# Two modulation blocks move from TensorE to VectorE, the gate's sums move into the feed-forward part, and the second output ends tile by tile

## The reference

```python
mod = c_act @ w_mod + b_mod          # c_act: 2048, w_mod: 2048 x 12288
mod_c = cc_act @ w_mod + b_mod
sh1, sc1, gt1, sh2, sc2, gt2 = split(mod, 6)
h = rmsnorm(x) * (1 + sc1) + sh1;  hc = rmsnorm(ctx) * (1 + csc1) + csh1
x = x + gt1 * merge_groups(scans(h, hc)) @ w_out
h2 = rmsnorm(x) * (1 + sc2) + sh2
x = x + gt2 * (silu(conv3x3(h2 @ w_gate)) * (h2 @ w_val)) @ w_down
return rmsnorm(x, g_final)
```

## Time and profile before

| | |
|---|---|
| median of 3 runs | 2120.66 us (2119.5 to 2120.87) |
| profiled execution | 2120.52 us, span 2118.7, mean granted clock 0.996 |
| PE busy | 2072.9 us, 98% of the span |
| DVE busy | 1599.7 us, 76% |
| ACT busy | 1034.8 us, 49% |
| POOL busy | 112.0 us, 5% |
| DMA | 501.47 MB, mean 237 GB/s |

### The profile page before, as it was taken

How to read it: one execution, slowest core, us unless ns; L and a number is a source line. 1 busy time by engine, 2 the same in 40 slices (tenths; PEclk the granted TensorE clock), 3 DMA queues, 4 the chain that set the end, 5 groups by cost and what they waited for, 6 DMA issues and landing times.

```text
span 2118.7 us, 29080 instructions
## 1 busy us (share of the span) xinstructions
PE 2072.9 (98%) x10157; PEld 1723.0 (81%) x10157; DVE 1599.7 (76%) x2385; ACT 1034.8 (49%) x1289; POOL 112.0 (5%) x175
## 2 busy tenths in 40 slices
PE   7999999999999999999999999999999999999998
PEld 6777778888887778887888887788888888878886
DVE  5789898867787887787666776578888888875554
ACT  4444445654444544546434555355555545544443
POOL 0011010110101110111000000000000000000000
PEclk9999999999999999999999999999999999999999
DMA  8998889998887999986444347565655656567664
GB/s 310 325 323 294 301 266 345 341 292 288 298 293 256 341 302 381 314 294 189 146 127 122 110 128 247 178 202 177 203 181 183 194 178 190 177 216 232 192 192 141
DMA packets 286328, 501.47 MB, mean 237 GB/s; under 512 B 22906, under 2 KB 114464, under 8 KB 284176
## 3 DMA queue, kind: packets, MB, share of 16 engines
q1 hardware_dynamic: 276320, 468.77, 66.9%
q0 software_dynamic: 9904, 31.32, 5.0%
HBM read 487.35 MB, written 19.75 MB: 239 GB/s over the span
## 4 chain that ended last, share of the span: by engine, by line
PE 51%; DVE 1%; DMA 1%; ACT 0%; issue 0%; ACTq 0%; DVEq 0%
PE gemm_ps L1999 23%; PE gemm_ps L2519 8%; PE ps L2519 7%; PE gemm_ps L2522 4%; PE ps L2522 4%; PE ps L2372 1%; PE ps L2441 1%; DMA w_raw<-in_w_out_dram 1%; DVE w_lo L1163 0%; PE ps L2395 0%; PE ps L2394 0%; PE ps L2355 0%; PE ps L2336 0%; PE ps L2067 0%; PE ps L2317 0%
## 5 line engine op out<-in xcount | busy, mean ns | idle before, releaser
L1163 DVE TENSOR_TENSOR w_lo<-w_raw,w_hi 128x1024 fp32r<-128x1024 f32 (+1 forms) x688 | 828.8, 1214 | 354.5 <-ACT w_hi L737 346.6
L737 ACT ACTIVATE w_hi<-w_raw 128x1024 fp32r<-128x1024 f32 (+1 forms) x688 | 717.3, 1053 | 614.4 <-PE gemm_ps L1999 243.3
L1999 PE MATMUL gemm_ps<-w_hi,a_both 128*128 128x512 f32 x2944 | 952.2, 396 | 11.5 <-DVE a_both L1203 6.2
L1999 PEld LDWEIGHTS gemm_ps<-w_hi,a_both 128*128 128x128 f32 x2944 | 554.5, 188 | 141.8 <-issue 12.9
L1999 PE MATMUL gemm_ps<-w_lo,a_both 128*128 128x512 f32 x1472 | 575.1, 391 | 0.0
L1999 PEld LDWEIGHTS gemm_ps<-w_lo,a_both 128*128 128x128 f32 x1472 | 277.6, 189 | 55.0 <-issue 1.0
L2519 PE MATMUL gemm_ps<-a_both,w_hi 128*128 128x512 f32 x704 | 193.8, 397 | 1.6 <-DVE a_both L1203 1.6
L2519 PE MATMUL ps<-a_both,w_hi 128*128 128x512 f32 x672 | 184.7, 394 | 0.0
L1901 DVE SCALAR_TENSOR_TENSOR acc<-gp,cw,acc 128x256 f32<-128x256 f32 x344 | 151.6, 481 | 19.8 <-ACT acc L1109 6.0
L1348 DVE SCALAR_TENSOR_TENSOR msum<-mraw,cs,msum 128x1024 f32<-128x1024 f32 x120 | 153.4, 1278 | 4.7 <-DMA mraw<-in_w_mod_dram 4.0
L1999 PE MATMUL gemm_ps<-w_hi,ft_hi 128*128 128x512 f32 x344 | 134.1, 390 | 3.2 <-DVE w_lo L1163 3.2
(11 more groups left out here) (437 smaller groups left out, 1770.5 us busy)
## 6 DMA issues: line engine op xcount, KB each, us to landing
w_raw<-in_w_in_dram SPq DMA_DIRECT2D x336, 512.0 KB, 5.0
mraw<-in_w_mod_dram SPq DMA_DIRECT2D x192, 512.0 KB, 6.7
w_raw<-in_w_up_dram SPq DMA_DIRECT2D x336, 256.0 KB, 3.0
w_raw<-in_w_down_dram SPq DMA_DIRECT2D x84, 512.0 KB, 4.3
w_raw<-in_w_out_dram SPq DMA_DIRECT2D x64, 512.0 KB, 5.6
w_raw<-in_w_up_dram SPq DMA_DIRECT2D x24, 512.0 KB, 5.7
fold_d<-msum POOLq DMA_DIRECT2D x8, 512.0 KB, 5.4
x_d<-xres POOLq DMA_DIRECT2D x2, 2048.0 KB, 9.1
```

Source lines behind the costliest of these rows:

```text
L737: act.activation(w_hi[:, slot, :, 0:n], raw[:, slot, :, 0:n], ACT.Copy).then_inc(hi_done, 1)
L1163: dve.tensor_tensor(w_lo[:, slot, :, 0:n], raw[:, slot, :, 0:n], w_hi[:, slot, :, 0:n].bitcast(F32), ALU.subtract).then_inc(lo_done, 1)
L1999: mm = pe.matmul(out[:, rt, 0:n], x[:, chunk0 + k, rt * P:(rt + 1) * P], w[:, slot, kk, 0:n], start=(k == 0 and part == 0), stop=(k == chu ...
```

## The change

1. Two instead of four two-row blocks on PE, so four halves of 16 matmuls instead of eight, spaced 21 units apart. Six on DVE: four beside the projections as before, the last two in the pair stage, in the places where sums 2 and 3 were, one block of eight loads and 32 operations for each sum of 16 loads and 16 operations.
2. Sums 2 to 5 in OUT, the context projections and the first x block; sums 6 and 7 in feed-forward blocks 3 to 18, two rows a block, with buffers and a kept copy of the activations of their own. The loops over feed-forward blocks are unrolled on SP and DVE (those of PE and ACT stay), and the pair loop on SP.
3. POOL's queue follows: all folds of the blocks of the pair stage come before the residual's load; sums 2, 3 and 4 before the low-rank weights (`wlr`); sums 6 and 7 and the gate's bias before the gate's load (`gt2b`).
4. OUT2's last block by tile, as at the kernel's end; `tile_root` in place of `roots`; ACT's and DVE's first two feed-forward units move around it.

The core of the diff:

```diff
-PE_MODS = 4
+PE_MODS = 2
+EARLY_BLOCKS = 4
-PAIR_SUMS = (2, 3)
+FFN_SUMS = (6, 7)
+FFN_FIRST = 3
...
-    places = [13 + 21 * h // 2 for h in range(2 * PE_MODS)]
+    places = [13 + 21 * h for h in range(2 * PE_MODS)]
...
-    first = {0: (99, 12), 1: (114, 13), 4: (8 * B_OUT + 8, 16), 5: (8 * B_CTX + 2, 17),
-             6: (8 * B_CTX + 22, 17), 7: (8 * B_X + 4, 18)}
+    first = {0: (99, 12), 1: (114, 13), 2: (8 * B_OUT + 13, 20), 3: (8 * B_CTX + 4, 20),
+             4: (8 * B_CTX + 27, 20), 5: (8 * B_X + 2, 18)}
...
+            def ffn_sum_unit(b, i):
+                at = 2 * (b + 1 - FFN_FIRST) + (i - 3) // 2
+                if i in (3, 5) and 0 <= at < 2 * KC:
+                    sum_unit(FFN_SUMS[at // KC], at % KC)
...
-            with sp.Fori(0, FB - 1) as i:
-                ffn_units(U_FFN // SLOTS + 2 * i, T * i, T)
+            for b in range(FB - 1):
+                ffn_units(U_FFN // SLOTS + 2 * b, T * b, T, lambda i: ffn_sum_unit(b, i))
...
             sum_store(0)
             sum_store(1)
             gate_bias(2)
-            sum_store(2)
-            sum_leaves(3)
+            row_store(4)
+            row_store(5)
             pool.wait_ge(evac_dve, 12)
             pool.dma_start(xres[:], xv).then_inc(S("xres_in"), 16)
...
-            sum_folds(3)
-            sum_store(4)
             pool.wait_ge(evac_dve, 16)
             pool.dma_start(x1_d, xres[:]).then_inc(S("x1_out"), 16)
-            sum_store(5)
-            sum_store(6)
+            sum_store(2)
+            sum_store(3)
+            sum_store(4)
...
+            for n in FFN_SUMS:
+                sum_store(n)
+            gate_bias(5)
             pool.dma_start(gt2b[:], mod_d[0, 0, 5 * D:6 * D].partition_broadcast(P)).then_inc(S("gt2_in"), 16)
...
             for rt in range(RT):
                 last_square(rt, xres, lambda rt: y[:, rt, (DC - 1) * NBLK:DC * NBLK], 1)
+                splits(U_FFN // SLOTS, rt, rt + 1, ffn=True)
+                act.wait_ge(S("root_out"), rt + 1)
+                for c in range(2):
+                    scaled_tile(rt, c)
...
-                    sum_row(PAIR_SUMS[0] + p // 4, at_unit // 2 - 2)
+                    block_rows(KC * (EARLY_BLOCKS + p // 4) + at_unit // 2 - 2)
...
+                if c == DC - 1:
+                    dve.wait_ge(S("tile_ps"), 1)
+                    last_block(0, xres, c % 2, gtb, sg)
+                    tile_root(0, 1)
+                    dve.engine_nop().then_inc(S("root_out"), 1)
+                    dve.wait_ge(used, U_OUT2 + BU * DC)
+                    last_block(1, xres, c % 2, gtb, sg)
+                    splits(U_FFN // SLOTS, 0, 1)
+                    tile_root(1, 1)
+                    dve.engine_nop().then_inc(S("root_out"), 1)
+                    splits(U_FFN // SLOTS, 1, 2)
+                    continue
...
-            sum_of_parts(1)
-            roots()
...
+                    at = 2 * (b - FFN_FIRST) + (i - 3) // 2
+                    if i in (3, 5) and 0 <= at < 2 * KC:
+                        sum_row(FFN_SUMS[at // KC], at % KC)
...
-            with dve.Fori(0, 9) as n:
-                me.iteration(first, 14 * n)
-                for k in range(2):
-                    ffn_block(2 * n + 2 + k, k)
+            for b in range(2, FB):
+                ffn_block(b, b % 2)
...
                 product(U_OUT2 + BU * c, 0, c % 2, a_hi, a_lo, BU, after=after,
-                        turning=("y", y, KC // 2) if c == 0 else None, ahead=Y_AHEAD)
+                        turning=("y", y, KC // 2) if c == 0 else None, ahead=Y_AHEAD, by_tile=SLOTS if c == DC - 1 else 0)
```

More of the change, by code:

```diff
@@ L173, in row_places @@
     ops, loads = {}, {}
-    steps = ROW_BLOCKS * KC
+    steps = EARLY_BLOCKS * KC
     at = [13 + 82 * j // steps for j in range(steps)]
@@ L199, in sum_places, with turn_of, OPS_AHEAD, LOADS_AHEAD @@
                 fetched = at[j - 4] + 4
-            elif n - 1 in first:
+            elif n - 1 in first and n != EARLY_SUMS:
                 fetched = max(first[n - 1][0] + (12 + j) * first[n - 1][1] // 16 + 4, start - 7 + j)
             else:
-                fetched = start - 6 + 2 * j if n == 0 else 8 * B_OUT + j
+                fetched = start - 6 + 2 * j if n == 0 else 8 * B_OUT + 4 + j
             loads.setdefault((fetched // 8, fetched % 8), []).append(16 * n + j)
     return ops, loads
-def MOD_OUT(m):
-    return 16 * (4 * m + 6 * (m - 1))
+EARLY_SUMS = 2
+MOD_OUT = {1: 16 * (6 + 4)}
+def turn_of(kind, n):
+    order = [("rows", m) for m in range(EARLY_BLOCKS)] + [("sum", m) for m in range(EARLY_SUMS)]
+    order += [("rows", m) for m in range(EARLY_BLOCKS, ROW_BLOCKS)] + [("sum", m) for m in range(EARLY_SUMS, SUMS)]
+    at = order.index((kind, n))
+    return order[:at]
+def OPS_AHEAD(kind, n):
+    return sum(ROW_OPS if k == "rows" else KC for k, _ in turn_of(kind, n))
+def LOADS_AHEAD(kind, n):
+    return sum(BU // SLOTS if k == "rows" else KC // SLOTS for k, _ in turn_of(kind, n))
+def LEFT(kind, n):
+    return 16 * (len(turn_of(kind, n)) + 1)
 MOD_AFTER, MOD_LOADS, MOD_COPIES = mod_places()
@@ L401, in build, with tile_of @@
     gbias_in, biased = S("gbias_in"), S("biased")
+    def tile_of(kind, n):
+        if kind == "rows":
+            return rsum[n % 2] if n < EARLY_BLOCKS else msum
+        return msum_ffn if n in FFN_SUMS else msum
     mod_in = [S(f"mod_in{i}") for i in range(BU)]
@@ L639, in sum_store @@
             def sum_store(n):
-                sum_leaves(n)
+                group_leaves("sum", n)
                 sum_folds(n)
@@ L1077, in _ @@
             for c in range(DC):
-                for i in range(2, 10):
+                for i in range(2, 8 if c == DC - 1 else 10):
                     if c == 0 and i - 2 >= Y_AHEAD:
@@ L1322, in block_rows @@
                 n, k = j // KC, j % KC
-                dve.wait_ge(mod_in[j // UK % SLOTS], 16 * (j // UK // SLOTS + 1))
-                row = mraw[:, j // UK % SLOTS, j % UK]
+                place, tile, ahead = k // UK % SLOTS, tile_of("rows", n), OPS_AHEAD("rows", n)
+                dve.wait_ge(mod_in[place], 16 * (LOADS_AHEAD("rows", n) + k // UK // SLOTS + 1))
+                row = mraw[:, place, k % UK]
                 if j == 0:
@@ L1343, in sum_row @@
                         dve.wait_ge(S("h_L"), 2 * HEADS)
-                    dve.wait_ge(sum_out, 16 * (ROW_BLOCKS + n))
-                    dve.tensor_scalar(msum[:], row, cs[:, j, 0:1], None, ALU.mult).then_inc(sum_used, 1)
-                else:
-                    dve.wait_ge(sum_used, ROW_BLOCKS * ROW_OPS + 16 * n + j)
-                    dve.scalar_tensor_tensor(out=msum[:], in0=row, scalar=cs[:, j, 0:1], in1=msum[:],
+                        dve.tensor_copy(cs_kept[:, :], cs[:, :, 0])
+                    dve.wait_ge(sum_out, LEFT(*turn_of("sum", n)[-1]))
+                    dve.tensor_scalar(tile[:], row, by, None, ALU.mult).then_inc(sum_used, 1)
+                else:
+                    dve.wait_ge(sum_used, ahead + j)
+                    dve.scalar_tensor_tensor(out=tile[:], in0=row, scalar=by, in1=tile[:],
                                              op0=ALU.mult, op1=ALU.add).then_inc(sum_used, 1)
```

141 lines of the change are left out of this document (74 added, 67 removed).

## The result

The changed kernel takes 2123.97 us in the median of 22 runs (2121.61 to 2126.81), the kernel before 2119.88 us beside it (22 runs): 1.0017 of it, 95% interval 1.0011 to 1.0024. So it is slower by some 4 us, within the 0.2% that was called no change, and above the range. The profiled execution has a span of 2121.0 us.

A forecast was written before the change was run, and what follows sets the result against it. PE was taken to bound the kernel nearly everywhere, with DVE near. Terms -7.7 (halves), -1.5 (second output's end), +3.8 (transposes) and 0 elsewhere gave -5.4: 2120.5 to 2115.1 us; range 2109.0 to 2121.9.

The forecast's parts named there:

- The prediction's own sign: Early stage: shrinking by less than 6 us would show the forecast wrong; some 7.7 us sooner would show it right.
- Part 1: Early projections and heads: four of eight modulation halves leave PE, 4 x 1.92 us, so -7.7 us; bounds 0 and -8.
- It counts in full only where PE is the bound. It is here: Early stage: the halves' whole 7.7 us is won, as PE is 98.6% busy and DVE gains no work there.
- Rival 2: No change within 0.2%: DVE gives back half of the early gain, the residual lands up to 3 us late; 2121.9 us; chance 0.27.
- The pair stage: Two blocks replace sums 2 and 3 there: 41 us more at most on DVE, which has 60 us free; cost 0.
- The transposes: Last column blocks of first output product and context projections: sum rows make DVE late; +3.8 us, bounds 0 and +6.3.
- POOL's queue before the first output product: Residual load issued later, near 686, landing just in time, against three fewer sum rows; 0, bounds -3 and +3 us.
- The later load of the low-rank weights on POOL: It falls into a stretch with ACT unhurried; cost 0.
- Rival 3: Slower: DVE becomes the bound in feed-forward blocks 3 to 18, +18 us, 2133 us; decides from 1.85 us a row; chance 0.08.
- The feed-forward part: Two rows a block bring DVE to 21.2 of 22.5 us, filling idle time; 0, upper bound +3 to +5 us.
- Part 3: Second output's end, tile by tile: PE goes on at +5.7 us instead of 7.2, so -1.5; bounds 0 and -3.8.
- a drain behind each operation: VectorE: by the skill a 1278 ns row would hold DVE some 2.3 us; set aside for the trace's 1.14 us.

The follow-up runs named there:

- Experiment 7: On experiment 1's kernel, VectorE's two-row operations beside projections and heads work on 32 of 512 columns from the second row on; 2109.3 us (0.9951).
- experiment 8: On experiment 3's kernel, three of VectorE's six two-row blocks lie early and three in the pair stage, instead of four and two; 2118.44 us (0.9996).
- experiment 3: Changed kernel with all of sum 2's store and folds ahead of the residual's 2 MB store on POOL; 2114.91 us (0.9978).
- experiment 5: On experiment 1's kernel, sums 2 and 4 packed into 13 and 15 units instead of 20, off the transposes; 2118.20 us (0.9991).
- experiment 6: On experiment 3's kernel, sums 2, 3 and 4 begin at units 296, 322 and 342, 18 units each; 2115.98 us (0.9986).
- experiment 10: On experiment 9's kernel, sum 4 packed into 15 units instead of 20, off x1's transposes; 2104.20 us (0.9926).
- experiment 4: Kernel before the change, with POOL storing the residual ahead of sum 4's store and folds; 2131.27 us (1.0052).
- experiment 1: Changed kernel with sum 2's transfer to DRAM issued before POOL waits for the residual and stores it, folds after; 2118.64 us (0.9988).
- experiment 2: Changed kernel with sum 2's transfer issued after POOL's wait for the residual but ahead of the residual's 2 MB store; 2122.08 us (1.0003).
- experiment 12: On experiment 3's kernel, each of the 32 rows in the feed-forward blocks is added twice on VectorE; 2136.19 us (1.0079).
- experiment 9: On experiment 8's kernel, the 48 pair-stage rows come 1.25 units apart instead of 1.5; 2107.26 us (0.9941).

## Why the prediction was wrong, point by point

The forecast was 2115.1 us, 5.4 us less; measured were 4 us more. Two steps failed: four halves were counted in full, and a store that moved on POOL was put at 0. The prediction's own sign, an early stage that shrinks by less than 6 us, came true.

- **Part 1 (-7.7): wrong in size.** -2.3 by the offsets. The step "It counts in full only where PE is the bound. It is here" failed. Each of the four halves does give its 1.5 to 2.1 us where it stood, at 93, 159, 227 and 296 us, 7.3 in all; but 5 us of it are handed back between 165 and 312 us, in waits for VectorE's `probsT`, `qkn` and low halves. PE at 98.6 of 100 us was taken for the bound, when PE and VectorE were both at their limits: as I read it, the halves had been the time in which VectorE caught up. Rival 2 had this mechanism, with half of the gain lost; it was 65 to 70%. Experiment 7 shows that VectorE was the bound, and experiment 8 with nothing left out. Thin rows win 12.3 us between 20 and 312 us, more than the four halves held, so VectorE had cost the kernel before some 5 us there already.
- **The pair stage (0): right.** The offset is -3.71 at 440 and -3.69 at 689 us.
- **The transposes (+3.8): right.** +1.8 and +1.8, by the working given. Experiments 3, 5, 6 and 10 show that this loss can be moved; sum 4's went for nothing, sum 2's came back in the output product.
- **POOL's queue before the first output product (0, -3 to +3): outside its bounds.** -4.6. The residual came in time; what counted was that the 16 rows of the kernel before began at unit 296, 1.0 a unit, and now begin at 301, 0.8 a unit: the 3.0 us that PE waited there for low halves are gone. Rows 2 showed the 4.7 us of waits that this could give back; I gave it half a sentence and no working. Experiment 6 loses nearly all of it again with an earlier start and 0.9 rows a unit; which of the two counts more is not shown.
- **The miss: +9.6, in no term.** For the first output product I followed POOL's queue load by load; for the context projections I stopped at "The later load of the low-rank weights on POOL falls into a stretch with ACT unhurried: 0". There sum 2's store had been put behind the wait for the residual and its store. The prediction names what is queued behind the residual's load but never who waits for the store of a sum: VectorE, in the first row of the next one, with all its low halves behind that row. The diff shows it in three lines, and the kernel before had the store of its sum ahead. Experiments 3 and 4 show it both ways: 8 to 9 us gone when the order is put back, 10.6 us more when it alone is put into the kernel before. Experiments 1 to 3 split the loss: 5 to 6 of the 9.6 us went when the sum's transfer was put ahead of the 2 MB, the rest when the 2 MB no longer lay beside the first loads of the context projections. Rival 3 was on the right side for another reason, and its place was quiet.
- **The feed-forward part (0): right.** No PE wait in blocks 3 to 18, and VectorE is busy for 21.1 us of such a block where 21.2 was worked out. Rival 3 would decide sooner than priced: by experiment 12 a block has room for about 1 us more, where VectorE idles 1.4.
- **Part 3 (-1.5): right in its wait, half in its worth.** 5.71 for 7.19, but 0.8 us went again in the matmuls behind it: the clock fell as expected, and is granted at half through 1380:1384 and on to 1388, where the kernel before has 0.50 in 1380:1384 and 0.70 in 1384:1388. The prediction gave the clock only a chance to win something (bound -3.8); it cost something.

With the order put right the kernel is at 2114.9, the forecast's own number, but that is luck: the terms differ, 5 us less from the halves, 4 to 5 us more from the output product.

The Trainium skill ("DMA: Bandwidth & Descriptors", section "Issuing engines are not separate DMA queues") says that transfers started by different engines run on the same DMA engines and interleave. The runs agree: ScalarE waited 6.9 us for a weight unit that SP had issued beside POOL's 2 MB store in experiment 1. With the store at 812 us it still waits 4.0 us for one (experiment 3), but PE waits nowhere from 806 to 830; that it had more units in hand there is likely and not shown.

The prediction quoted the Trainium skill ("VectorE: DVE Perf Modes", section "The DRAIN you can't avoid") for a drain behind each operation. The same paragraph of the page goes on that a next operation which is not held (kept back until the ones ahead have finished) starts earlier, which the prediction left out. So the trace's 1.14 us need not contradict the page.

What stays open: why the clock falls at 950 us. Of the 2.6 us won between 900 and 1306 us some 1.0 is a wait of PE for VectorE's `a_both` at 1303 us, 1.1 us long in the kernel before, which the changed kernel's trace does not have. The other 1.6 is a fall of the granted clock in the trace of the kernel before:

```profile
950.00:955.00 5.00, 5.00 (x17) 3.94 (x17) 4.28 (x11) 0.00 (x0) 0.00 (x0) 0.71 1.01 362
```

PE had not waited in the 50 us ahead of it; right before, from 946.13 to 948.97, it did 24 matmuls of four columns each. The changed kernel does the same 24 and keeps the full clock. Of the 14 traces 8 have a granted clock under 1.00 in 900 to 980 us (the kernel before and experiments 1, 2, 4, 6, 8, 9 and 10) and 6 do not, so I do not count the 1.6 us for the change; no run tells why.

## What to carry to other kernels

When a store moves on a queue, ask who waits for the buffer that it empties, and what is queued behind that wait, as carefully as who reads what it stores: a 2 MB store, and the wait for it, put ahead of a 512 KB one cost 8 to 11 us in a kernel of 2120. Where two engines are both near 90 to 99% busy, taking work from one gives back only what the other can follow; here moving a quarter of VectorE's rows out of that stretch was worth 9 us there (8 on the whole, once the pair stage's rows were placed well), and removing four of PE's eight modulation halves 2. And idle time is not all slack: of the 1.4 us that VectorE had idle in a feed-forward block, about 1 could be used.

## What was not expected of the hardware

- The order of two transfers on one queue counted: 512 KB issued 0.7 us behind 2 MB took 11.9 us; issued 0.55 us ahead of it (experiment 2), 5.1.
- A stall of 6.4 us on PE cost 3.0 us more in matmuls at the lower clock, almost half as much again. Behind the stall of 9.7 us in experiment 4 they cost 1.6, so a longer stall need not cost more.
- In the kernel before the clock fell at 950 us without any wait of PE in the 50 us ahead of it, and 8 of 14 traces show such a fall.
